# The last group of each feed-forward with its early products ahead of the second weight chunk, and bias tables added up in PSUM

## What is computed

```python
def conv_ffn(x, w_up, conv_w, conv_b, w_down):      # layers 0 and 1 of the first block
    h = x @ w_up
    h = lax.conv_general_dilated(h, conv_w[:, None, :], ...) + conv_b
    a, g = jnp.split(h, 2, axis=-1)
    return (jax.nn.silu(g) * a) @ w_down

def swiglu(h, w_gu, w_down):                        # twice in each layer of the second block
    g, u = jnp.split(h @ w_gu, 2, axis=-1)
    return (jax.nn.silu(g) * u) @ w_down

def t5_bucket(rel):                                 # 32 buckets, edges grow with the distance
    ...
    bias = rel_table[t5_bucket(rel)]                # sliding-window attention, 6 heads
```

## Time and profile before

| | |
|---|---|
| median of 3 runs | 4423.28 us |
| lowest and highest | 4421.26 and 4425.78 us |
| the profiled execution, own time | 4422.46 us |
| its span | 4420.7 us |
| mean granted TensorE clock | 0.935 |
| busy: TensorE / VectorE / ScalarE / GpSimd | 88% / 47% / 33% / 35% |

### The profile page before, as it was taken

The page is one execution under the profiler, slowest core; times in us unless marked ns, Lnnn a source line. Parts: engine busy times, 40 slices in busy tenths (PEclk is TensorE's granted clock), DMA queues, the critical chain, the costliest instruction groups (busy, mean ns, idle before and its releaser), DMA issues. The chain is left out here.

```text
span 4420.7 us, 51623 instructions
## 1 busy us (share of the span) xinstructions
PE 3896.3 (88%) x18724; PEld 3021.0 (68%) x18724; DVE 2089.4 (47%) x3587; ACT 1448.8 (33%) x2238; POOL 1546.3 (35%) x756
## 2 busy tenths in 40 slices
PE   6777889999788879999998677899999988778999
PEld 3775678888666658867886443688778866337887
DVE  4817877443545675645445756322232232552222
ACT  2216232222326533333223254322232233443222
POOL 1221134444130135543553211355444532104454
PEclk8989999999989989999999887999999998789999
DMA  6430124442110136744662110133322321102332
GB/s 206 144 76 18 56 95 133 140 134 63 34 43 1 37 105 211 229 137 152 219 226 78 48 33 1 53 96 97 92 77 90 100 74 54 29 1 67 95 95 72
DMA packets 459779, 409.76 MB, mean 93 GB/s; under 512 B 30063, under 2 KB 404975, under 8 KB 459631
## 3 DMA queue, kind: packets, MB, share of 16 engines
q1 hardware_dynamic: 457183, 406.50, 30.1%
q10 hardware_dynamic: 2448, 1.32, 0.1%
HBM read 404.10 MB, written 7.60 MB: 93 GB/s over the span
## 5 line engine op out<-in xcount | busy, mean ns | idle before, releaser
L198 POOL TENSOR_TENSOR s_wlo<-s_raw,s_whi 128x1024 fp32r<-128x1024 f32 x490 | 1180.9, 2417 | 2233.6 <-ACT s_whi L190 2233.2
L212 PE MATMUL psum<-s_xhi,s_whi 128*128 128x512 f32 x3264 | 1239.9, 380 | 121.3 <-DVE s_xlo L421 69.5
L213 PE MATMUL psum<-s_xlo,s_whi 128*128 128x512 f32 x3264 | 1230.8, 377 | 0.0
L214 PE MATMUL psum<-s_xhi,s_wlo 128*128 128x512 f32 x3264 | 1225.5, 375 | 0.0
L190 ACT ACTIVATE s_whi<-s_raw 128x1024 fp32r<-128x1024 f32 x490 | 508.8, 1054 | 1809.2 <-PE psum L214 1753.3
L212 PEld LDWEIGHTS psum<-s_xhi,s_whi 128*128 128x128 f32 x3264 | 621.7, 190 | 251.3 <-issue 135.8
L213 PEld LDWEIGHTS psum<-s_xlo,s_whi 128*128 128x128 f32 x3264 | 621.6, 190 | 114.7 <-issue 4.5
L214 PEld LDWEIGHTS psum<-s_xhi,s_wlo 128*128 128x128 f32 x3264 | 620.0, 190 | 114.4
L212 PE MATMUL psum<-s_ahi,s_whi 128*128 128x512 f32 x1232 | 481.3, 391 | 32.8 <-POOL s_wlo L198 22.7
L213 PE MATMUL psum<-s_alo,s_whi 128*128 128x512 f32 x1232 | 472.8, 384 | 0.0
L214 PE MATMUL psum<-s_ahi,s_wlo 128*128 128x512 f32 x1232 | 472.4, 383 | 0.0
(11 more groups left out here) (229 smaller groups left out, 4288.4 us busy)
## 6 DMA issues: line engine op xcount, KB each, us to landing
s_ada_raw<-w_ada SPq DMA_DIRECT2D x224, 512.0 KB, 3.8
s_raw<-w_gu SPq DMA_DIRECT2D x176, 512.0 KB, 3.9
s_raw<-w_up SPq DMA_DIRECT2D x88, 512.0 KB, 4.7
s_raw<-w_dn SPq DMA_DIRECT2D x88, 512.0 KB, 3.5
s_raw<-w_down SPq DMA_DIRECT2D x44, 512.0 KB, 4.6
s_raw<-w_in SPq DMA_DIRECT2D x28, 512.0 KB, 3.9
s_raw<-w_in_ab SPq DMA_DIRECT2D x20, 512.0 KB, 6.1
s_area<-w_first SPq DMA_DIRECT2D x16, 512.0 KB, 11.9
```

Of the source, the lines that this page charges most:

```text
L198: pool.tensor_tensor(K.wlo[:, c % HL, 0:a * b], K.raw[:, c % RAW, 0:a * b], K.whi[:, c % HL, 0:a * b].bitcast(F32), ALU.subtract).then_inc ...
L212: pe.matmul(out, lh, rh, start=first, stop=False)
L213: pe.matmul(out, lh, rl, start=False, stop=False)
L214: return pe.matmul(out, ll, rh, start=False, stop=last)
```

## The change

In the last group of a feed-forward (j = GRP) TensorE waits for the first down chunk alone, makes the products q = 0 of several tiles (5 at 512 tokens, 3 at 768), then waits for the second chunk and makes q = 1 of each tile; the remaining tiles follow with both. In other groups the order stays. The `BiasTable` sums are held in banks 6 and 7 of PSUM, behind the waits of `settled` (three semaphores), and are copied to the tables at the end by one instruction each; the last copy gives `bias_ready`.

```diff
             if j > 0:
                 e.wait_ge(self.sem["act_lo"], self.at("act_lo", 2 * j + n * 4))
-                ws = [chunk_ops(K, e, self.down_chunk_of(j, q), n) for q in range(2)]
                 b = (j - 1) % 2
+
+                def down(m, q, ws):
+                    for a, w in parts(T):
+                        ins = three(e, self.slot(T, self.down_tile(j, m))[:, a:a + w],
+                                    (ws[0][:, 0, m * P:(m + 1) * P], ws[1][:, 0, m * P:(m + 1) * P]),
+                                    (K.ahi[:, b, q, a:a + w], K.alo[:, b, q, a:a + w]), q == 0, q == 1)
+                    return ins
+
+                first = chunk_ops(K, e, self.down_chunk_of(j, 0), n)
+                early = 0 if j < GRP else self.ring(T) - (T == TX)
+                for m in range(early):
+                    self.take_n(e, self.down_tile(j, m), n)
+                    down(m, 0, first)
+                second = chunk_ops(K, e, self.down_chunk_of(j, 1), n)
                 for m in range(8):
-                    i = self.down_tile(j, m)
-                    self.take_n(e, i, n)
-                    for q, (wh, wl) in enumerate(ws):
-                        for a, w in parts(T):
-                            ins = three(e, self.slot(T, i)[:, a:a + w],
-                                        (wh[:, 0, m * P:(m + 1) * P], wl[:, 0, m * P:(m + 1) * P]),
-                                        (K.ahi[:, b, q, a:a + w], K.alo[:, b, q, a:a + w]), q == 0, q == 1)
-                    ins.then_inc(self.sem["out_ready"], 1)
+                    if m >= early:
+                        self.take_n(e, self.down_tile(j, m), n)
+                        down(m, 0, first)
+                    down(m, 1, second).then_inc(self.sem["out_ready"], 1)
                     if j == GRP and self.norm:
                         self.norm.sum(e, m - 2)
...
     def __init__(self, K, heads, tables):
         self.pos, self.heads, self.tables = K.pos_i, heads, tables
+        self.sums = [K.pf[:, (6 + i) * BANK:(7 + i) * BANK] for i in range(len(heads))]
...
         for i, h in enumerate(self.heads):
-            ins = e.tensor_scalar(self.tables[i], rel, 0.0, tab[:, h, 0:1], ALU.mult, ALU.add)
+            ins = e.tensor_scalar(self.sums[i], rel, 0.0, tab[:, h, 0:1], ALU.mult, ALU.add)
...
         e.wait_ge(self.sem["x_ready"], self.at("x_ready"))
+        self.settled(e)
         self.distances(e)
-        rel, mask, acc = K.t2[:, 0, 0:TX], K.t2[:, 1, 0:TX], self.tables
+        rel, mask, acc = K.t2[:, 0, 0:TX], K.t2[:, 1, 0:TX], self.sums
...
-        e.sem_inc(self.sem["bias_ready"], 1)
+        for table, total in zip(self.tables, acc):
+            ins = e.tensor_copy(table, total)
+        ins.then_inc(self.sem["bias_ready"], 1)
```

## The result

The changed kernel takes 4380.01 us, the median of four runs (4377.90 to 4384.59), beside 4422.75 us for the kernel before. The ratio is 0.9901, 95% interval 0.9888 to 0.9914, so 42.7 us less; 4375 us with 4366 to 4389 was predicted. The profiled execution took 4380.49 us with a span of 4377.4 us, 43.3 less than before's 4420.7.

A forecast was written before the change was run, and what follows sets the result against it. TensorE, the longest lane, was taken as the bound, losing time standing still or running slowly. Last groups 34.7 plus bias tables 12.9 gave 47.6 us off 4422.46; adjusted to the median, 4375 us, range 4366 to 4389.

The forecast's parts named there:

- last group, 768 tokens: Last group of the feed-forward at 768 tokens: three early tiles cover 3.15 of 3.8 us waiting; 4.7 us gained.
- three with sums: Last groups of three feed-forwards followed by a PreNorm, whose sums stand between the tiles: 5.7 us each, 17.1 gained.
- table A: Bias stretch from 90 us, one table: sums in PSUM avoid stalls; 1.8 us gained, all counted.
- table B: Bias stretch from 469 us, two tables: about 6 us gained on DVE, 1.4 counted, since a factor comes late.
- table C: Bias stretch from 1524 us, one table: accumulations in PSUM no longer stall; 3.7 us gained, all counted.
- table D: Bias stretch from 2421 us, two tables: accumulations in PSUM no longer stall; 6.0 us gained, all counted.
- The rival of the falling clock: Last groups: the clock falls even behind the short pause; 15 us less gain, 4390 us; chance 0.10.
- fell only near their end: Last groups: mean clock 0.90 over the 3.8 us wait, so it fell late and a 0.33 us pause keeps it.
- a split that begins in the accumulations lets on average 0.72 us run on: Two-table bias step: splits beginning in accumulations (76%) gain 0.72 us, those in the mask 1.45; 0.90 on average.
- The rival of dearer PSUM: Bias tables: PSUM makes accumulations dearer; 9.3 us less gain, 4384 us; chance 0.08.
- the slower one: Bias stretches from 90, 1524 and 2421 us: TensorE's writes hold up DVE in PSUM; 4468 us; chance 0.02.
- All counts: Bias stretch from 90 us: SP's copy and ACT's Silu rows wait for the table, so its whole 1.8 us counts.

The follow-up runs named there:

- busy pause: Changed kernel with one tile ahead in every last group, its first-chunk products made five times (three at 768 tokens) so TensorE keeps running; 4394.57 us, ratio 0.9934.

## Why the prediction was right, and where its terms were off

| term | predicted, us | measured in the trace of after, us |
|---|---|---|
| last group, 768 tokens | 4.7 | 4.67 |
| convolved, 512 tokens | 6.45 | 6.25 |
| three with sums | 17.1 | 5.49 + 5.63 + 5.82 = 16.9 |
| last | 6.45 | 6.34 |
| table A | 1.8 | 0.1 kept; late clock -2.1 |
| table B | 1.4 | 1.34 |
| table C | 3.7 | 2.35 |
| table D | 6.0 | 4.7 |
| sum | 47.6 | 40.6, of 43.3 |

**The last groups** went by the steps of the prediction: fifteen products ahead, a pause of 0.3 us, the clock kept in every trace with the full number of early tiles, DVE caught up by the last tile. 34.2 us of 34.7. The rival of the falling clock is refuted at this length of pause.

The reason that the prediction gave for the clock was weaker than its outcome. That the clock "fell only near their end" was read as a delay behind the standstill, of which 0.33 us would be a tenth. In the 24 full pauses of four traces it fell 2.2 to 5.3 us after TensorE had stopped, in seven of them only when TensorE ran again. Nor has a full pause one price: the third group with sums took 22.19 us in one trace of before and 21.01 in the other, and the six groups together 124.0 and 123.1 us there, 121.9 in the traces of the tables alone and of A alone. Against these the early products give 32 to 34 us; that the trace from which the prediction was made, and against which the table above is measured, had the dearest six is luck.

**Bias tables, the step that failed** is "a split that begins in the accumulations lets on average 0.72 us run on", that is, the gain per split taken as a mean over a random phase. Stalls in D were 16.8 us before (74.14 from first to last mask, less 57.3). They are 10.3 in the changed kernel (67.6 less 57.3), so 6.6 were gained where 7.75 was predicted. In C they went from 16.8 to 13.7, 3.1 in place of 4.6. Where splits come evenly the phase isn't random, since the chain falls in step with them: in C, with a step of 1.25 us and a period of 5.44, a stall of 1.69 is left in every period, where the mean gave 2.1 - 0.54 = 1.56; in the second half of D it is 5.44 - 2 x 1.91 = 1.62, where the mean gave 2.1 - 0.90 = 1.2. The stalls ahead of these vary (0.6 to 2.2), without a rule that the runs show. The costs of PSUM were right: copies of 0.69, 1.3 for two in D, and 0.27 more for a first value, where 0.2 was put; the accumulations 4 ns dearer, with their overlap kept (1.42 a pair). The rival of dearer PSUM is refuted, and so is the slower one, DVE held up by TensorE in PSUM. C gave 2.35 us in four traces with the changed tables and 3.6 in three others, one step of 1.25 apart: in the three a free step fits in between the second split and the third, and the mask that meets the third takes 1.7 us in place of 2.5 to 2.7.

**B** was capped as said: the table is 7.7 us shorter, but the factor it waits for came when it did, and 1.34 was left, in every trace with B shorter.

**A** was expected to be on the path. It is, for some 10 us, to the row that ACT waited for; what follows are weight loads that don't start earlier. In the timed runs A alone gave nothing (ratio 1.0003). The step that failed is "All counts".

**The rest**, 2.7 us in favour, is the granted clock at other places, both ways, and that it came out in favour is luck. Behind the group at 768 tokens it is worse: the windows over the start of the `Norm` of the kernel before,

```profile
1154.00:1160.00 6.00, 3.02 (x12) 1.76 (x11) 5.29 (x5) 4.30 (x5) 4.20 (x2) 1.00 0.00 0
1160.00:1166.00 6.00, 6.00 (x20) 3.34 (x19) 0.49 (x1) 3.76 (x6) 0.47 (x1) 1.00 0.00 0
```

and of the changed kernel,

```profile
1152.00:1158.00 6.00, 3.02 (x10) 2.00 (x9) 5.11 (x5) 3.51 (x5) 4.02 (x2) 0.88 0.00 0
1158.00:1164.00 6.00, 6.00 (x17) 3.12 (x16) 0.66 (x1) 3.33 (x4) 0.64 (x1) 0.84 0.00 0
```

show the same 3 us of idle time ahead of the squares' sums (3.02 busy of 6.00) passed over at 1.00 before, and followed by 0.84 after; 1.7 us of the 4.7 go back there, in each of the traces with fewer or all tiles early but the one with the busy pause, where none went back. The tables alone and A alone, without early products, lost 2.6 us there, the two traces of before nothing: again the same idle time, passed over or not. At the `Norm` behind the convolved group the changed kernel gains 2.8 us more, in both of its traces.

In the attention of the last layer, from 3800 to 4100 us, the first trace gains another 6.1 us. The windows over the same products in the kernel before, in the changed kernel and in its second trace:

```profile
3823.00:3829.00 6.00, 5.11 (x20) 3.07 (x17) 0.00 (x0) 1.75 (x4) 0.00 (x0) 0.50 0.00 0
...
3792.00:3798.00 6.00, 4.98 (x24) 2.50 (x20) 0.00 (x0) 2.82 (x6) 0.00 (x0) 1.00 0.00 0
...
3788.30:3794.30 6.00, 5.11 (x20) 3.10 (x17) 0.00 (x0) 1.78 (x4) 0.00 (x0) 0.50 0.00 0
```

The second trace of the changed kernel has no such gain. Two others have it whole (the mask alone in PSUM, and all but A). Again the place of the clock's changes against the program goes with it: on the time of the kernel before, the clock fell at 3819.1 us in these three traces, at 3818.7 to 3818.8 in the nine that gained nothing, and at 3817.5 to 3817.6 in the two that gained 0.7 and 0.8. By the last of ScalarE's instructions the first trace of the changed kernel is 36.9 us ahead of before's, the second 34.6. Two traces of before, the same program, lie 4.5 us apart at 2860 us. Other stretches of the changed kernel's first trace take back some 4.5 us together, 2.6 of them between 2600 and 2860 us. A difference of 2 us in one trace and one stretch with half-speed products can therefore be put down to no edit without a further trace.

## What to carry to other kernels

Work that needs only the first of two late inputs can be put ahead of the wait for the second. Here it paid 1.6 times the 21.5 us of waiting that it took away, since a TensorE that goes on keeps its clock; it needn't cover the wait wholly, a rest of 0.3 us cost just that. Where VectorE and GpSimd share the load, give every instruction of a long VectorE chain one operand in PSUM, an input if it has two, and choose the tile that costs least: one scratch tile, here the mask, did more than two sum tiles with their copies. Price stalls against a partner that comes at even distances by the remainder of its period over your step, not by a mean over phases. And before you give 2 us in one trace a cause, look at where the granted clock changed in it.

## What the runs showed of the hardware that was not expected

- A one-input mask with its output in PSUM takes 0.695 us, with its input there 0.691, against 0.428 in SBUF, and neither is ever held up by POOL's split (155 masks in two kernels).
- A chain of steps on VectorE falls in step with GpSimd's splits: periods of 5.44 us, stalls of 1.68 us with steps of 1.25, and of 1.29 with steps of 1.39.
- A pause of TensorE of 2.3 to 3.1 us is followed by 1.2 GHz in four cases of ten; equal pauses of 3.03 us differ by 2.8 us in what they cost. Behind pauses of 3.8 to 4.0 us the clock fell 2.2 to 5.3 us after TensorE had stopped, in 7 of 24 when it ran again.
- The clock of the same program rose at 344 or at 351 us, and the attention of the last layer was 6.1 us shorter or not. In both places a few tenths of a microsecond in where the clock's changes lie against the program go with the outcome, in all fourteen traces.
